# A decoder layer on one core: attention matmuls in plain fp32 on halves of the array, in place of split operands

## The reference, cut to what matters

```python
h = rms_norm(x, pre_g)
cb, cc, ch, cz, q, k, v, sz, mq, mz = split(h @ w_in)     # 4 x 384, 384, 128, 128, 384, 256, 256
y_conv = cb * conv3(cc * ch) * silu(cz)
# sliding window of 128, 6 query heads on 2 key heads, head size 64
s = q @ k.T / 8 - slope * dist          # outside the window -1e30
p = softmax(concat([s, sink]))[..., :-1]
y_swa = (p @ v) * silu(sz)
# 4 heads on 256 memory tokens, no position, no sink
y_mem = (softmax(mq @ mk.T / 8) @ mv) * silu(mz)
y = x + rms_norm(concat([y_conv, y_swa, y_mem]) @ w_out, post_g)
```

## Time and profile before

| | |
|---|---|
| median of 3 runs | 1045.18 us (1044.28 to 1045.58) |
| the profiled execution | 1045.22 us, span 1043.4 us, mean granted TensorE clock 0.959 |
| PE busy | 923.5 us, 89% |
| DVE, ACT, POOL busy | 548.1, 390.6, 479.9 us |
| DMA | 114.67 MB, mean 110 GB/s |

### The profile page before, as it was taken

One profiled execution on the slowest core, in us unless ns is written; L12 is line 12 of the kernel. 1 busy time (PEld: TensorE's weight loads), 2 busy tenths in 40 slices (PEclk: granted clock), 3 DMA queues, 4 the chain that ended last, 5 costly groups with the idle time before them and its releaser, 6 DMA issues.

```text
span 1043.4 us, 12781 instructions
## 1 busy us (share of the span) xinstructions
PE 923.5 (89%) x4872; PEld 787.6 (75%) x4872; DVE 548.1 (53%) x1033; ACT 390.6 (37%) x1045; POOL 479.9 (46%) x279
## 2 busy tenths in 40 slices
PE   1978699789999999798999998888999989989895
PEld 1878689789787878576787877776777877767784
DVE  4662456566745354574637344664563635646513
ACT  4422563543313255444222236454231235444411
POOL 2435334334675254253667434433545644433462
PEclk9999799999999899999999899998999999989998
DMA  9421322111626222211635502221352421211152
GB/s 330 139 81 62 128 89 89 41 61 62 253 91 235 108 81 81 81 61 46 239 111 192 182 21 87 74 101 62 116 192 81 153 99 62 73 48 61 61 182 81
DMA packets 40109, 114.67 MB, mean 110 GB/s; under 512 B 6000, under 2 KB 12656, under 8 KB 39632
## 3 DMA queue, kind: packets, MB, share of 16 engines
q1 hardware_dynamic: 40048, 113.86, 31.4%
HBM read 104.61 MB, written 10.25 MB: 110 GB/s over the span
## 4 chain that ended last, share of the span: by engine, by line
PE 53%; DVE 23%; ACT 16%; issue 4%; DMA 2%; POOL 1%; SPq 1%; POOLq 0%; DVEq 0%; ACTq 0%
PE pj L521 32%; PE pa L521 16%; ACT prob L920 4%; ACT prob L821 3%; PE pa L609 3%; DVE mx L1340 2%; DVE prob L1337 2%; DVE c_t L1208 1%; ACT mprob L821 1%; ACT y_hi L821 1%; DVE c_t L1206 1%; DVE mpt_lo L1080 1%; DVE g_t L1226 1%; ACT mprob L933 1%; DVE o_sum L1383 1%
## 5 line engine op out<-in xcount | busy, mean ns | idle before, releaser
L492 POOL TENSOR_SCALAR w_hi<-w_raw 128x1024 fp32r<-128x1024 f32 x132 | 143.5, 1087 | 482.1 <-PE pj L521 405.0
L521 PE MATMUL pj<-h_hi,w_hi 128*128 128x512 f32 (+1 forms) x960 | 349.5, 364 | 8.0 <-DVE q_bd L1167 5.3
L521 PE MATMUL pj<-h_lo,w_hi 128*128 128x512 f32 (+1 forms) x960 | 345.5, 360 | 0.0
L521 PE MATMUL pj<-h_hi,w_lo 128*128 128x512 f32 (+1 forms) x960 | 344.5, 359 | 0.0
L493 POOL TENSOR_TENSOR w_lo<-w_raw,w_hi 128x1024 fp32r<-128x1024 f32 x132 | 326.1, 2471 | 11.0
L521 PEld LDWEIGHTS pj<-h_hi,w_hi 128*128 128x128 f32 x960 | 187.5, 195 | 34.2 <-issue 6.3
L521 PEld LDWEIGHTS pj<-h_hi,w_lo 128*128 128x128 f32 x960 | 186.2, 194 | 26.0
L521 PEld LDWEIGHTS pj<-h_lo,w_hi 128*128 128x128 f32 x960 | 187.0, 195 | 23.2
L920 ACT ACTIVATE prob<-prob,nmx 128x256 f32<-128x256 f32 x96 | 47.5, 497 | 85.1 <-DVE sexp L1343 85.1
L1080 DVE TENSOR_TENSOR pt_lo<-pa,pt_hi 128x512 fp32r<-128x512 f32 x48 | 30.2, 684 | 87.5 <-ACT pt_hi L821 87.5
L521 PE MATMUL pa<-w_hi,y_hi 128*128 128x512 f32 x160 | 63.5, 397 | 0.0
(11 more groups left out here) (217 smaller groups left out, 1429.2 us busy)
## 6 DMA issues: line engine op xcount, KB each, us to landing
w_raw<-in_weights SPq DMA_DIRECT2D x132, 512.0 KB, 3.4
res<-in_x_prompt SPq DMA_DIRECT2D x16, 512.0 KB, 7.1
out_y_prompt<-o_nat SPq DMA_DIRECT2D x16, 512.0 KB, 5.7
x_row<-in_x_prompt SPq DMA_DIRECT2D x12, 512.0 KB, 3.6
x_t<-in_xt SPq DMA_DIRECT2D x12, 512.0 KB, 6.6
first_rows<-in_x_prompt SPq DMA_DIRECT2D x4, 512.0 KB, 5.8
x_t<-in_xt SPq DMA_DIRECT2D x8, 256.0 KB, 5.6
mkt_s<-in_mkt SPq DMA_DIRECT2D x2, 1024.0 KB, 5.8
```

The costliest lines, as they stand in the source:

```text
L492: need(step(pool.tensor_scalar(w_hi[slot][:], w_raw[slot][:], 1.0, 1.0, ALU.mult, ALU.mult)))
L521: return pe.matmul(out, lhsT, rhs, start=start, stop=stop)
```

## The change

- Queries, keys, values and probabilities of both attentions are kept unsplit in fp32 (`q_sb`, `k_sb`, `v_sb`, `mq_sb`, `mk_sb`, `mv_sb`, `pt`, `mpt`). A score is one matmul of contraction 64 on the upper or the lower 64 rows of the array; values are one matmul per key head and key tile with 64 output columns, on the left or right half of the columns, and land already summed and in place in one bank. The columns of `w_in` and rows of `w_out` are put in an order on the host in which a query tile holds a head of each key head.
- ACT alone evacuates the K, Q and M tiles, with the scale 1/8 in its copy; DVE's subtractions go, as do the high copies.
- One `tensor_tensor_reduce` for a head adds the bias to the negated score and takes the minimum; the sink stands as a 257th score, so that the exponential's sum holds it.
- The division by the sum goes from ACT (six copies) to DVE (three `tensor_tensor` on pairs of heads, their reciprocals ahead of them), at 4 steps after the scores in place of 6 (memory: two, at 3 in place of 4). Maximum, exponential, division, turn and copy are handed on by pairs of heads. Values come one step earlier (13 and 10 after the scores).
- The samples' values have probabilities as the stationary operand (32 columns, on four strips) and the cached values as the moving one; three transposes turn the result.
- Three slots for weight tiles in place of two; the squares of the next quarter's rows are taken by ACT three tiles earlier.

The core of the diff (the places in the queues, TensorE's and VectorE's new functions):

```diff
+WS = 3
 def freed_by_act(name):
-    return name[0] == "V" or name[:2] in ("CC", "MK")
+    return name[0] in "VKQM" or name[:2] == "CC"
-SW_V = {key: s + 14 for key, s in SW_S.items()}
+SW_V = {key: s + 13 for key, s in SW_S.items()}
-MM_V = {key: s + 11 for key, s in MM_S.items()}
-SM_S, SM_T, SM_V = 14, 22, 27
+MM_V = {key: s + 10 for key, s in MM_S.items()}
+SM_S, SM_T, SM_V, SM_O = 14, 22, 27, 30
+PLACE = [0, 1, 3, 4, 2, 5]
+SCORES = [5, 0, 3, 1, 4, 2]
             def split(n):
-                slot = n % 2
+                slot = n % WS
...
-                    pool.wait_ge(proj_done, last_unit(SEQ[n - 2]))
+                    pool.wait_ge(proj_done, last_unit(SEQ[n - WS]))
             def sample_values(q):
...
-                    mm(pa[4][:, r], v_c[:, s, :], pt_s[:, r], True, False)
-                    mm(pa[4][:, r], vn_t[q - 1][:], ptn_s[:, r], False, True)
+                    mm(pa[4][r, 0:P], pt_s[:, r], v_c[:, s, :], True, False)
...
+                    mm(pa[4][r, 0:P], ptn_s[:, r], vn_t[q - 1][:], False, True)
+                for kt in range(2):
+                    for s in range(GS):
+                        r = slice(32 * s, 32 * s + 32)
+                        last = mm(pa[4][r, P:3 * P], mpt_s[:, kt, r], memv_c[:, kt, s, :], kt == 0, kt == 1)
             def swa_scores(q, i):
...
-                    pe.wait_ge(sw_taken, NBLK * q + i)
-                for h in range(NH):
-                    out = pa[h // 2][:, (h % 2) * 2 * W:(h % 2 + 1) * 2 * W]
-                    for n, keys in enumerate((k_hh, k_ll)):
-                        last = mm(out, q_st[:, h, i * P:(i + 1) * P], keys[:, h // G, i * P:i * P + 2 * W], n == 0,
-                                  n == 1)
+                    pe.wait_ge(sw_y32, NBLK * q + i)
+                for n, h in enumerate(SCORES):
+                    r, place = HALF_OF[h // G], PLACE.index(h)
+                    if h == 2:
+                        pe.wait_ge(sw_s, NH * (NBLK * q + i) + 1)
+                    mm(pa[place // 2][:, (place % 2) * 2 * W:(place % 2 + 1) * 2 * W],
+                       q_sb[r, h % G, i * P:(i + 1) * P], k_sb[r, i * P:i * P + 2 * W], True, True).then_inc(sw_s, 1)
             def swa_values(q, i):
+                pe.wait_ge(sw_pt, 3 * (NBLK * q + i + 1))
+                for kt in range(2):
+                    for kv in range(NKV):
+                        last = mm(pa[1][HALF_OF[kv], 0:G * P], v_sb[:, i + kt, kv, :],
+                                  pt[:, kv, kt, :, :].rearrange("p a b -> p (a b)"), kt == 0, kt == 1)
             def swa_exp(q, i):
+                for a in range(3):
+                    act.wait_ge(sw_max, 3 * (NBLK * q + i) + a + 1)
+                    for h in (2 * a, 2 * a + 1):
+                        last = act.activation(prob[:, h, 0:2 * W + 1], s_sb[:, h, 0:2 * W + 1], ACT.Exp,
+                                              bias=nmx[:, h:h + 1], scale=-1.0, accum_out=den[:, h:h + 1])
+                    last.then_inc(sw_exp, 1)
             def swa_max(q, i):
...
+                        last = dve.tensor_tensor_reduce(
+                            out=out, in0=pa[a][:, e * 2 * W + keys.start:(e + 1) * 2 * W], in1=bias[:, h, keys], scale=-1.0,
+                            scalar=s_sb[:, h, 2 * W:2 * W + 1], op0=ALU.add, op1=ALU.min, accum_out=nmx[:, h:h + 1])
+                    last.then_inc(sw_max, 1)
+            def swa_norm(q, i):
+                for a in range(3):
+                    hs = slice(2 * a, 2 * a + 2)
+                    dve.wait_ge(sw_exp, 3 * (NBLK * q + i) + a + 1)
+                    need(step(dve.reciprocal(rden[:, hs], den[:, hs])))
+                    dve.tensor_tensor(prob[:, hs, 0:2 * W], prob[:, hs, 0:2 * W],
+                                      rden[:, hs].unsqueeze(2).to_broadcast([P, 2, 2 * W]), ALU.mult).then_inc(sw_p, 1)
             def swa_y32_of(q, i):
+                dve.wait_ge(sw_pv, NBLK * q + i + 1)
+                dve.scalar_tensor_tensor(out=o_sum[:], in0=pa[1][:, 0:G * P].rearrange("p (g t) -> p g t", g=G),
+                                         scalar=0.5, in1=gate[:, 0:3, i * P:(i + 1) * P], op0=ALU.mult,
+                                         op1=ALU.mult).then_inc(sw_y32, 1)
```

More of the change, by code:

```diff
@@ L303, in layer @@
         xt_loaded = [sem(f"xt_loaded{i}") for i in range(8)]
[L304 removed]
+        w_loaded = [sem(f"w_loaded{s}") for s in range(WS)]
         cache_loaded = sem("cache_loaded")
@@ L662, in mem_values @@
+            def mem_values(q, i):
+                pe.wait_ge(mm_pt, 2 * (NBLK * q + i + 1))
+                p = i % 2
+                for kt in range(2):
+                    for hh in range(2):
+                        a = (2 * p + hh) * HD
+                        last = mm(pa[4][HALF_OF[hh], 0:2 * P], mv_sb[:, kt, a:a + HD],
+                                  mpt[:, hh, kt, :, :].rearrange("p a b -> p (a b)"), kt == 0, kt == 1)
                 last.then_inc(mm_pv, 1)
@@ L904, in v_hi @@
                     act.wait_ge(carried, q)
-                for b in range(NBLK):
-                    last = copy(v_st[:, 1 + b, :, 0:HD], pa[2][:, b * P:(b + 1) * P].rearrange(
-                        "p (v d) -> p v d", v=NKV))
-                last.then_inc(v_his, 1)
+                if q == 0:
+                    for g in range(2):
+                        copy(vn_t[g][:], pa[3][0:TG, g * P:(g + 1) * P])
+                copy(v_sb[:, 1:1 + NBLK, :, :].rearrange("p b v d -> p (b v d)"), pa[2][:]).then_inc(nat_out, 1)
             def sample_exp(q):
@@ L922, in swa_exp @@
-                act.activation(sexp[:], sexp[:], ACT.Exp).then_inc(sw_exp, 1)
-            def swa_norm(q, i):
-                act.wait_ge(sw_den, NBLK * q + i + 1)
-                for h in range(NH):
-                    last = copy(prob[:, h, :], prob[:, h, :], rden[:, h:h + 1])
-                last.then_inc(sw_p, 1)
-            def mem_exp(q, i):
-                act.wait_ge(mm_max, NBLK * q + i + 1)
-                for u in range(4):
-                    last = act.activation(mprob[:, u, :], pa[3 + u // 2][:, (u % 2) * NM:(u % 2 + 1) * NM], ACT.Exp,
-                                          bias=nmmx[:, u:u + 1], scale=SCALE, accum_out=msums[:, u:u + 1])
-                last.then_inc(mm_exp, 1)
@@ new lines, in mem_exp, with swa_pt @@
+            def mem_exp(q, i):
+                for hh in range(2):
+                    act.wait_ge(mm_max, 2 * (NBLK * q + i) + hh + 1)
+                    for u in (2 * hh, 2 * hh + 1):
+                        last = act.activation(mprob[:, u, :], pa[3 + hh][:, (u % 2) * NM:(u % 2 + 1) * NM], ACT.Exp,
+                                              bias=nmmx[:, u:u + 1], accum_out=msums[:, u:u + 1])
+                    last.then_inc(mm_exp, 1)
+            def swa_pt(q, i):
+                for a, out in enumerate((pt[:, 0, :, 0:2, :], pt[:, 1, :, 0:2, :], pt[:, :, :, 2, :])):
+                    act.wait_ge(sw_turned, 3 * (NBLK * q + i) + a + 1)
+                    turned = pa[a][:].rearrange("p (e k b) -> p e k b", e=2, k=2)
+                    copy(out.rearrange("p k e b -> p e k b") if a < 2 else out, turned).then_inc(sw_pt, 1)
@@ L969, in y_memory, with mem_pt @@
+            def mem_pt(q, i):
+                for hh in range(2):
+                    act.wait_ge(mm_turned, 2 * (NBLK * q + i) + hh + 1)
+                    copy(mpt[:, hh, :, :, :].rearrange("p k t b -> p (k t b)"), pa[3 + hh][:]).then_inc(mm_pt, 1)
             def y_memory(q):
@@ L1579, in laid_out @@
 def laid_out(a):
-    w_in, w_out = a["w_in"][0], a["w_out"][0]
+    pairs = np.concatenate([np.arange(h * HD, (h + 1) * HD) for g in range(G) for h in (g, G + g)])
+    cols, rows = np.arange(24 * P), np.arange(D)
+    for at_ in (OFF["Q"], 5 * DC + 2 * P):
+        cols[at_:at_ + DC] = at_ + pairs
+    rows[DC:2 * DC] = DC + pairs
+    w_in, w_out = a["w_in"][0][:, cols], a["w_out"][0][rows]
     tiles = [w_in.reshape(KT, P, 24, P).transpose(2, 1, 0, 3).reshape(24, P, D),
```

460 lines of the change are left out of this document (150 added, 310 removed).

## The result

The changed kernel takes 930.54 us (median of 4 runs, 930.48 to 930.89) against 1045.38 us for the kernel before in the same session (1044.28 to 1047.53): a ratio of 0.89, 95% interval 0.8884 to 0.8915.

What follows compares the result with a forecast made beforehand. PE, busy 89% of the span, bounds the kernel, losing time to waits and a lowered clock. 1045.2 - 78 (stalls) - 28 (clock) - 7 (streams) + 36.5 (shape changes) - 7.5 (samples) = 961, predicted 960 us; 8-in-10 range 932 to 1004.

Steps and rivals of the forecast that it cites:

- stalls: PE's waits in the attentions and for a Q tile, 86.2 us in all: shorter chains remove 78 us.
- clock: Attention stretches at mean granted clock 0.95: without long stalls and narrow matmuls, 28 us come back; bounds 0 and 32.
- streams and changes of shape: Attention blocks on PE: 7 us off for unsplit fp32 passes, 36.5 us added for switching between array shapes.
- samples' values: Swapped operands cut the narrow matmuls of the samples' values, 3.8 us in each of two quarters: 7.5 us saved.
- Changes between array shapes: Each half-array section costs 0.57 us of emptying and unhidden weight loads, four a block, 16 blocks: +36.5 us; bounds +14, +51.
- Streams: Attention matmuls in plain fp32 with both array halves at work: 4.25 us a block for 4.7, 7 us off over 16 blocks.
- in turn: Rival, 9%: the array's halves work one after the other in attention's scores and values, 1029 us.
- slower: Rival, 6%: attention's halves work one after the other and each weight load is bare, +129 us, 1090 us.
- weight loads of a half aren't hidden: Rival, 8%: each of the 18 passes of a half shows its weight load, +24 us, 984 us.
- The shared port: Rival, 13%: DVE's new divisions wait up to 2.6 us for POOL, PE's waits return in half their size: +40, 1000 us.
- Nothing for the third slot: Third weight slot gains nothing, since PE hardly waits for POOL; if POOL's split were late, worth one tile.
- Nothing for the lighter load of ScalarE and VectorE: ACT's and DVE's lighter load as such gains nothing, both being under 56% busy in the attention stretch.

Runs made afterwards that it cites:

- the third experiment: Changed kernel with the samples' values made as before (cached values as the 128-column stationary operand, 32 moving columns, no turn of the result): 945.21 us, ratio 0.9043.

## Why the prediction missed, by its own steps

The sum against the measured change of 114.7 us in the span; what was measured is worked out from starts of matmuls, by the same rule as above (beyond pace by over 0.3 us).

| step | predicted, us | measured, us |
|---|---|---|
| stalls | -78 | -90 (107.1 before, 17.4 after) |
| clock | -28 | about -32 (0.95 to 1.00 in all four stretches) |
| streams and changes of shape | -7 + 36.5 = +29.5 | +16.5 |
| samples' values | -7.5 | about -8.7 |

The third line is worked out from the medians of the sections: a block's four cost 1.43 + 1.40 + 0.94 + 0.95 = 4.73 before and 1.70 + 1.64 + 1.26 + 1.21 = 5.81 after, 17.3 for 16 blocks, less 0.2 in each of four places where a window's values and memory scores touch. The last is the third experiment's 7.8, less 1.2 for its half clock, against 2.24, twice.

- **Changes between array shapes: the term that failed.** 0.57 us was read from one section whose entry held about 0.15 us that have nothing to do with the shape, since the same section takes 1.63 before and 1.49 after. I then added a few hundredths for wider loads; the halves of the rows are at 0.41, those of the columns at 0.36. 64 sections at 0.18 less are 11.5 us, and the four pairs that touch save another 0.8. The mechanism was right as far as the lengths tell (emptying and bare weight loads, two such lengths at each change where my low bound had one). My bounds of 0.22 and 0.8 held it, the value taken inside them did not.
- **Stalls.** Right in place, and in mechanism but for the longest: short chains, no wait in attention. The 11.2 us wait of quarter 0 I had put down to the chain that only just fits, but 6.9 us between its exponentials and its division are the split of the memory's keys (the run with later turns has the lines). So the term holds about 7 us that went for another reason than the one I gave, and that part of the number is luck. I left 8 us for the place behind the convolution and a Q tile; it was in time by 0.16 us. The chain there was 12.05 and not 13.5 long, mainly since the memory's two divisions took 0.69 each there, where I had used the mean of 1.28. And the whole was 3.5 us larger than my 86.2. Together 12 us.
- **Clock.** Right, and 4 us better: with neither long stalls nor the narrow run it stayed at 2.4 GHz. Both causes were shown singly: the narrow run without a stall, stalls without the narrow run.
- **Streams.** Right: halves of rows and of columns run side by side, a pass of 256 columns in 0.216 a half. So "in turn" and "slower" fall, and "weight loads of a half aren't hidden" falls too, since passes of one half follow each other at 0.216 with a load each and no room for it. The Trainium skill, "TensorE: Matmul & The Clock Gate", Part 3, says that weight loads overlap a matmul only on other rows, and that matmuls start strictly in program order; here neither held, the second by the seventh pass that starts with the third.
- **The shared port.** The rival's mechanism is real and its price was right (up to 2.76 us where I had 2.6): 17 divisions overlapped POOL's subtraction, none of them ahead of the copies that have 0.16 us to spare. What failed is its step from there to PE, +40 us: with division on ScalarE, which has no such long ones, the time is the same. The Trainium skill, "GPSIMD Engine Reference", section 1, names two SBUF inputs as a case of contention; the trace agrees, and gives the price.
- **Nothing for the third slot:** wrong by 4 us, inside what the stalls' term measured. **Nothing for the lighter load of ScalarE and VectorE** is wrong too: both are idle half of the time, and still their split of the memory's keys held PE up, by its place in the queues.
- **The range.** 12 us of stalls, 4 of clock, 13 of sections and 1 of samples, 30 in all, are all errors to one side. The bounds of the single terms would have held it (the sections 22 us cheaper, no stall and no half clock left: 961 - 22 - 8 - 4 = 927), but my low end was 932.

What removed the stalls: no part alone. Without the pairs 11 us come back, with a long reduction 21, with early turns 31, and places alone give the old kernel 20 of 115. The copies behind the convolution have 0.16 us to spare, so a longer chain ahead of them shows at once, and the numbers are no shares of a sum. What the lighter queues by themselves gave was not tried apart; the longest stall shows that they gave something.

## What to carry to other kernels

A price read from one section of the trace is taken with its entry compared to other entries; a stray 0.15 us, times 64, was a third of the error. Where TensorE changes the array's shape, count each pair of changes (here 0.36 to 0.41 us) and put sections of one shape together, and look for who is late next (here an in-order queue that stood in another engine's wait). Before a part of a change is given credit, see how much time the chain has to spare behind it: the division's engine was worth nothing, the hand-on by pairs 11 us. And when a wait names an operation, list what stands in its queue between that operation and its inputs: here 6.9 us of it was other work.

## What was not expected of the hardware

- The passes of one half that stood behind six of the other began when only three of those were still ahead in the order; behind four, they began at once (0.013 us). So the order in the program mattered (8.7 us) only beyond that.
- 32 matmuls of 32 columns, each with a load of 128, brought the clock down to 0.51 for 6.8 us without any wait of PE. In the versions of the changed kernel without them, and past the first 30 us, PE's waits of 3.2 to 4.1 us brought it down for 3.4 to 6.9 us each time, those of 2.6 to 2.8 us (the run with two reductions) in three of four, those of up to 2.1 us never. In the kernel before, a wait of 3.4 us did not and two of three waits of 1.9 us did, so the length of a wait alone doesn't decide it.
- A division of 128x512 with both operands in SBUF that began during POOL's subtraction ended 0.55 us after it, as if it had begun only with its end (342.39 + 2.38 = 344.77, the division to 345.31). So a mean such as the 1.28 of the earlier trace rows is no duration that any one of them has.
- A fused addition and minimum on 128x256 took 0.48 us by its record but 0.405 from start to start.
